# Decode rows' memory attention moved into the sixteenth projection block, and the block end ahead of the attention removed

## The reference, cut to what matters

```python
def mem_branch(p, mk, mv, dtype):
    B, L, _ = p['mem_q'].shape
    q = p['mem_q'].reshape(B, L, MEM_H, MEM_DH).astype(F32)
    s = jnp.einsum('blhd,bmhd->bhlm', q, mk.astype(F32)) * (MEM_DH ** -0.5)
    a = jax.nn.softmax(s, axis=-1)
    o = jnp.einsum('bhlm,bmhd->blhd', a, mv.astype(F32)).reshape(B, L, MEM_W)
    return (o * jax.nn.silu(p['mem_z'].astype(F32))).astype(dtype)

# for the decode rows: c_s = mem_branch(ps, c_mk, c_mv, x_s.dtype)
#   c_mk, c_mv: 8 x 256 x 4 x 128;  ps['mem_q']: 8 x 4 x 512
```

## Time and profile before

| | us |
|---|---|
| median of 3 runs | 2792.88 |
| lowest, highest | 2790.41, 2792.89 |
| the profiled execution's own time | 2791.27 |
| its span | 2789.4 |
| PE busy | 2710.3 (97%) |
| stretch from the last product of quad 15 to `dots(0)` | 39.50, PE busy 25.07 |

### The profile page before, as it was taken

One profiled execution on the slowest core, in us unless ns is written; L12 is line 12 of the kernel. 1 busy time (PEld: TensorE's weight loads), 2 busy tenths in 40 slices (PEclk: granted clock), 3 DMA queues, 4 the chain that ended last, 5 costly groups with the idle time before them and its releaser, 6 DMA issues. The chain is left out here.

```text
span 2789.4 us, 35948 instructions
## 1 busy us (share of the span) xinstructions
PE 2710.3 (97%) x13915; PEld 1927.5 (69%) x13915; DVE 1244.9 (45%) x2147; ACT 580.6 (21%) x1367; POOL 404.6 (15%) x819
## 2 busy tenths in 40 slices
PE   7998999999999999999999999999789999899998
PEld 6674468856844588888888888888655565455553
DVE  3252688867854663142222144451232232345453
ACT  3122458760000000000010100100132232122221
POOL 0000014320000000000000023320123200333341
PEclk9999999999999999999999999999899999999999
DMA  6457312212222221222342354552764411875652
GB/s 228 107 160 247 110 36 71 85 38 67 84 80 89 83 64 55 72 68 89 106 127 65 104 155 138 156 173 75 237 214 140 130 50 47 288 237 166 209 164 92
DMA packets 273463, 342.00 MB, mean 123 GB/s; under 512 B 40989, under 2 KB 226325, under 8 KB 268013
## 3 DMA queue, kind: packets, MB, share of 16 engines
q1 hardware_dynamic: 239932, 262.65, 30.1%
q0 software_dynamic: 16288, 67.46, 7.9%
q10 hardware_dynamic: 17072, 9.58, 1.1%
HBM read 262.16 MB, written 80.01 MB: 123 GB/s over the span
## 5 line engine op out<-in xcount | busy, mean ns | idle before, releaser
L1420 PE MATMUL sbank<-w,xT 128*128 128x256 f32 x3200 | 698.6, 379 | 0.0
L1420 PEld LDWEIGHTS sbank<-w,xT 128*128 128x128 f32 x3200 | 606.5, 190 | 85.0 <-issue 3.3
L1420 PE MATMUL sbank<-w,area 128*128 128x256 f32 x1664 | 361.3, 379 | 0.0
L1839 DVE TENSOR_TENSOR pout_b<-pout_b,sbank 128x256 f32<-128x256 f32 x320 | 134.2, 421 | 503.6 <-PE sbank L1420 414.8
L1420 PEld LDWEIGHTS sbank<-w,area 128*128 128x128 f32 x1664 | 315.9, 190 | 42.8
L1802 DVE TENSOR_TENSOR w<-w 128x2048 f32<-128x2048 f32 x63 | 142.8, 2288 | 320.7 <-PE sbank L1420 257.5
L1512 ACT ACTIVATE pout_b<-sbank 128x256 f32<-128x256 f32 x120 | 45.4, 384 | 890.0 <-PE sbank L1420 657.9
L1420 PE MATMUL sbank<-w 128*128 128x256 f32 x832 | 181.8, 379 | 2.6 <-issue 2.6
L1420 PEld LDWEIGHTS sbank<-w 128*128 128x128 f32 x832 | 158.0, 190 | 24.2 <-issue 2.8
L1417 PE MATMUL sbank<-xT,w 128*128 128x512 f32 x384 | 166.6, 593 | 0.0
L1417 PEld LDWEIGHTS sbank<-xT,w 128*128 128x128 f32 x384 | 72.7, 190 | 90.1 <-issue 90.0
(11 more groups left out here) (455 smaller groups left out, 3433.4 us busy)
## 6 DMA issues: line engine op xcount, KB each, us to landing
w<-in_w_in SPq DMA_DIRECT2D x64, 1024.0 KB, 5.3
proj<-pout_b SPq DMA_DIRECT2D x208, 128.0 KB, 1.7
area<-in_x_prompt SPq DMA_DIRECT2D x16, 1024.0 KB, 7.4
attention_then_units<-proj SPq DMA_DIRECT2D x128, 128.0 KB, 3.1
area<-roped_q_of_decode POOLq DMA_DIRECT2D x32, 256.0 KB, 4.1
w<-in_w_out SPq DMA_DIRECT2D x4, 2048.0 KB, 15.6
y_of_groups_b_c<-out_parts SPq DMA_DIRECT2D x32, 256.0 KB, 2.3
mo_dec_states<-in_state_mlstm_C SPq DMA_DIRECT2D x32, 256.0 KB, 5.9
```

What stands on the lines that cost most here:

```text
L1420: last = nc.tensor.matmul(bank[t][:, 0:256], x(c, t * P, (t + 1) * P), at[name][:, c, :], start=first_ and c == 0, stop=c == 7, skip_group ...
L1839: nc.vector.tensor_tensor(out[:, t, :], x[:, t, :], product_at(n, t), ALU.add).then_inc(sums_read, 1)
```

## The change

1. `select`, `attend_bc` and `mix_out` now share one block. The meeting of all engines between `select` and `attend_bc` is gone; instead SP, once the stores of quad 15 have landed except the last four, clears the stage's semaphores and increments `selected`, for which every engine waits.
2. Turning the decode rows' memory keys, their dots and the softmax move into quad 15: `decode_memory(step)`, after step 10 to 23 of it, on PE, ACT and DVE. SP loads the queries and the first four sequences' keys ahead of quad 15's stores, the other four after phase 2, and the values of all eight sequences through the rest of the quad.
3. The products with the memory values are cut in four (`memory_values(part)`), one behind `dots(s)` in each of slots 0 to 3. Slot 3's increments `closed`.
4. The decode logits and their softmax are spread over slots 2 to 5 (`decode_logits`, `decode_max`, `decode_p`, `decode_spread`); the tile is cleared in slot 0.
5. SP's queue: `load(0)` comes first, with `v` (2048 KB) and `mv` (512 KB) between its selection bias and its two gate tiles `z`; `load(1)` now stands behind the first part of `w_out`, and this behind `closed`. New ids, head mask, `qr` and `kn` go through GpSimd's queue, ahead of its gathers.

The diff, cut:

```diff
-        bank = [k.ps(f"sbank{j}", [P, 512], st) for j in range(8)]
+        bank = [k.ps(f"sbank{j}", [P, 512], st) for j in range(6)] + k.banks
...
-                sp.dma_start(dst, qout[:, t, :]).then_inc(quad_out[t], 16)
+                sp.dma_start(dst, qout[:, t, :]).then_inc(last_out if (n, kind) == (NQ - 1, 3) else quad_out[t], 16)
...
             def quad(n):
+                if n + 1 == NQ:
+                    sp.wait_ge(r_stored, 16 * N_TILES)
+                    sp.dma_start(dmq, k.headT[:, T_MQ:T_MQ + H, SEQ:TOK]).then_inc(dmq_in, 16)
+                    sp.wait_ge(dots_s, 2 * NS)
+                    for b in range(4):
+                        load_keys(b)
...
                     sp.dma_start(k.mk, outs["prompt_mem_k"].rearrange("(c p) n -> p c n", p=P)).then_inc(k.mk_in, 16)
-                    for b in range(5):
-                        sp.dma_start(k.mkd[:, b, :, :], ins["cache_mem_k"][b].rearrange("(c p) n -> p c n", p=P)
-                                     ).then_inc(k.mkd_in[b], 16)
+                    for b in range(4, DEC_B):
+                        load_keys(b)
+                    load_values(7)
...
                 if n + 1 == NQ:
-                    for b in range(2):
-                        sp.dma_start(k.mvd[:, 2 * b:2 * b + 2, :], ins["cache_mem_v"][b].rearrange("(c p) n -> p c n", p=P)
-                                     ).then_inc(k.mvd_in, 16)
+                    load_values(0)
+                    load_values(1)
...
+                if n + 1 == NQ:
+                    load_values(2)
+                    load_values(3)
+                    sp.wait_ge(mkd_turned, 5)
+                    load_values(6)
...
                 if n + 1 == NQ:
-                    sp.wait_ge(r_stored, 16 * N_TILES)
+                    load_values(4)
+                    load_values(5)
                     sp.dma_start(k.kT, k.headT[:, T_K:T_K + H, 0:SEQ]).then_inc(k.keys_in, 16)
...
-                if n + 1 == NQ:
-                    sp.wait_ge(product, 28 * n + 28)
-                    sp.dma_start(k.v, outs["prompt_v"].rearrange("(c p) n -> p c n", p=P)).then_inc(k.keys_in, 16)
...
-            stored_by(NQ)
...
+            def dots_mkd(b):
+
+                if b == 0:
+                    pe.wait_ge(dmq_set, 2)
+                pe.wait_ge(mkd_kept_a, b + 1)
+                pe.wait_ge(mkd_kept_v, b + 1)
+                for h in range(H):
+                    last = nc.tensor.matmul(bank[7][NS * h:NS * (h + 1), 0:N_MEM], dmq_of[:, h, NS * b:NS * (b + 1)],
+                                            mkdT[:, b % 2, h, :], start=b == 0, stop=b == DEC_B - 1)
+                last.then_inc(mdots, 1)
+
+            def decode_memory(step):
+
+                b = step - MEMORY_AT
+                if 0 < b <= DEC_B:
+                    dots_mkd(b - 1)
+                if 0 <= b < DEC_B:
+                    turn_mkd(b)
+                if b == DEC_B + 3:
+                    pe.wait_ge(pm_ready, 1)
+                    for c in range(2):
+                        last = nc.tensor.transpose(bank[5][:, c * P:(c + 1) * P], pmd[:, c * P:(c + 1) * P], k.ident[:])
+                    last.then_inc(pm_turned, 1)
+                if b == DEC_B + 5:
+                    pe.wait_ge(pm_set, 4)
...
+                        if n + 1 == NQ:
+                            decode_memory(4 * phase + t)
...
+                if 0 <= b < DEC_B:
+                    dve.wait_ge(mkd_turned, b + 1)
+                    if b >= 2:
+                        dve.wait_ge(mdots, b - 1)
+                    nc.vector.tensor_copy(mkdT[:, b % 2, 2:4, :].rearrange("p a b -> p (a b)"), bank[6][:, :]
+                                          ).then_inc(mkd_kept_v, 1)
+                if b == DEC_B + 1:
+                    dve.wait_ge(mdots, DEC_B)
+                    of_memory.step(nc.vector.tensor_reduce(stat[:, 0:1], bank[7][:, 0:N_MEM], AX, ALU.max))
+                    nc.vector.tensor_scalar(stat[:, 1:2], stat[:, 0:1], -SCALE, None, ALU.mult).then_inc(pm_max, 1)
+                    nc.vector.memset(flat[:, 14336:16384], 0.0).then_inc(spread_clear, 1)
...
+        @block.sync
+        def _(sp):
+            for t in range(4):
+                sp.wait_ge(quad_out[t], 64 * NQ - 16)
+            sp.wait_ge(decode_out, 64 * NQ)
+            k.clear(sp)
+            sp.sem_inc(k.selected, 1)
...
             def load(t):
                 rows, u = slice(t * P, (t + 1) * P), t % 2
+                if t == 0:
+                    sp.wait_ge(selected, 1)
                 sp.dma_start(qT[:, u, :, :], k.headT[:, T_Q:T_Q + H, rows]).then_inc(loaded[u], 16)
                 sp.dma_start(mq[:, u, :, :], k.headT[:, T_MQ:T_MQ + H, rows]).then_inc(loaded[u], 16)
+                sp.dma_start(bias[:, u, 0:(t + 1) * P], k.sel[rows, 0:(t + 1) * P]).then_inc(loaded[u], 16)
+                if t == 0:
+                    sp.dma_start(v, outs["prompt_v"].rearrange("(c p) n -> p c n", p=P)).then_inc(v_keys_in, 16)
+                    sp.dma_start(mv[:, :, :], outs["prompt_mem_v"].rearrange("(c p) n -> p c n", p=P)).then_inc(mv_in, 16)
                 for j, c in enumerate((C_SZ, C_MZ)):
                     sp.dma_start(z[:, u, j, :], k.proj[rows, c:c + HW]).then_inc(loaded[u], 16)
-                sp.dma_start(bias[:, u, 0:(t + 1) * P], k.sel[rows, 0:(t + 1) * P]).then_inc(loaded[u], 16)
-
-            sp.dma_start(dmq[:, :, :], k.headT[:, T_MQ:T_MQ + H, SEQ:TOK]).then_inc(dmq_in, 16)
-
...
-            sp.dma_start(hm[:], ins["head_pick"][:, :]).then_inc(small_in, 16)
-            sp.dma_start(qr[:], k.sq.rearrange("t (h d) -> (t h) d", h=H)).then_inc(small_in, 16)
-            sp.wait_ge(k.new_stored, 16 * 2 * DEC_T)
-            for t in range(DEC_T):
-                sp.dma_start(kn[:, t, :], k.kn4[t].rearrange("b t (h d) -> (b t h) d", h=H)).then_inc(small_in, 16)
-            for b in range(5, DEC_B):
-                sp.wait_ge(mkd_turned, b - 4)
-                load_mkd(b)
-            for t in range(DEC_T):
-                sp.dma_start(vn[:, t, :], k.vn4[t].rearrange("b t (h d) -> (b t h) d", h=H)).then_inc(vn_in, 16)
-            for b in range(2, DEC_B):
-                sp.dma_start(mvd[:, 2 * b:2 * b + 2, :], ins["cache_mem_v"][b].rearrange("(c p) n -> p c n", p=P)
...
-                             ).then_inc(mvd_in, 16)
-            sp.dma_start(mv[:, :, :], outs["prompt_mem_v"].rearrange("(c p) n -> p c n", p=P)).then_inc(mv_in, 16)
+
             load(0)
...
                 sp.dma_start(w[b], ins["w_out"][ML_W:D, cs].rearrange("(c p) n -> p c n", p=P)
                              ).then_inc(w_in[b], 16)
+                if b == 0:
+                    load(1)
+                    for t in range(DEC_T):
+                        sp.dma_start(vn[:, t, :], k.vn4[t].rearrange("b t (h d) -> (b t h) d", h=H)).then_inc(vn_in, 16)
             for s in slots:
...
+            for t in range(DEC_T):
+                nc.gpsimd.dma_start(kn[:, t, :], k.kn4[t].rearrange("b t (h d) -> (b t h) d", h=H)).then_inc(small_in, 16)
             for q in range(QUADS):
...
+            def memory_values(part):
+                if part == 0:
+                    pe.wait_ge(k.mvd_in, 16 * DEC_B)
+                for b in (2 * part, 2 * part + 1):
                     for c in range(2):
-                        last = nc.tensor.transpose(
...
-            pe.wait_ge(keys_in, 32)
-            pe.wait_ge(mv_in, 16)
+            pe.wait_ge(keys_in, 16)
             for s in slots:
                 if 1 <= s <= A_UNITS:
                     turn_p(s - 1)
                 if s < A_UNITS:
                     dots(s)
+                if s < 4:
+                    memory_values(s)
                 if group(s) is not None:
                     multiply(group(s), 0)
                 if 2 <= s <= A_UNITS + 1:
...
                     turn_h(s - 2)
                 if 1 <= s <= A_UNITS:
                     mix(s - 1)
+                if s == 3:
+                    turn_logits()
...
                     finish_m(s)
+                if s == 0:
+                    nc.vector.memset(spread[:], 0.0).then_inc(masks, 1)
+                if s == 4:
+                    memory_out()
+                if s == 2:
+                    decode_logits()
+                if s == 3:
+                    decode_max()
+                if s == 4:
+                    decode_p()
+                if s == 5:
```

More of the change, by code:

```diff
@@ L1529, in quad @@
                     keep_groups(q)
+                if n + 1 == NQ:
+                    for step in range(MEMORY_AT, 16):
+                        decode_memory(step)
                 for kind in (2, 3, 4):
@@ L1984, in _ @@
             load(0)
-            load(1)
+            sp.wait_ge(k.last_out, 64)
+            sp.wait_ge(mk_turned, 1)
             sp.wait_ge(closed, 1)
@@ L2116, in _, with turn_logits @@
-            last.then_inc(closed, 1)
+            def turn_logits():
+                pe.wait_ge(lk_ready, 1)
+                for c in range(2):
```

(24 more changed lines are left out.)

370 lines of the change are left out of this document (183 added, 187 removed).

## The result

The changed kernel takes 2808.16 us (median of 5 runs, 2803.16 to 2810.99) where the kernel before takes 2792.89 (median of 5, 2790.41 to 2797.33). The ratio is 1.0053, with a 95% interval of 1.0038 to 1.0068: slower by some 15 us. A second set of five gave 2804.83 and a ratio of 1.0045 (1.0029 to 1.0060). The profiled execution took 2803.16 us, its span is 2801.3.

A forecast was written before the change was run, and what follows sets the result against it. PE, busy for 97% of the span, was taken to bound the kernel, with DMA late in some stretches. 13.0 - 21.0 + 12.3 + 2.0 = +6.3 us gave 2797.6, and 1.6 up to the median gave 2799.2; range 2789 to 2806.

The forecast's parts named there:

- the landing of `load(0)`: Between quad 15's last product (E) and `dots(0)`: its last tile lands 16.7 us after the first issue, bounds 14.2 and 19.5.
- `load(0)` alone: SP's queue up to the last gate tile: 3648 KB at 393 GB/s, 9.5 us, some 10.1 with short rows, plus 2.3 start.
- GpSimd's small loads: Beside `load(0)`: 450 KB in 1280 short pieces add 1.8 us to its landing.
- GpSimd's gathers: 8 x 256 KB, first issued at E + 8.2, meeting up to the last 4.5 us of `load(0)` and stretching these to double.
- quad 15: Eight sequences' key transposes and dots, plus softmax-weight transposes, cost PE their full time: +13.0 us, bounds 12.9 and 14.
- last product to `dots(0)`: From E, the end of quad 15's last product, to `dots(0)`: 18.5 us against 39.5, so -21.0, bounds -23.5 and -18.2.
- slots 0 to 2, length: Memory values partly at half clock and clearing in slot 0: 16.0 us against 13.6 before, bounds 12.9 and 17.5.
- slots 4 and 5, length: Two more transposes and softmax 0.6 us, half clock after the wait 1.4: +2.0 on 9.2, bounds +0.6 and +3.3.
- The second wait: In slot 3, `dots(4)` waits for `load(1)` behind `w_out`: 13.8 us after `dots(3)`, 3.9 before; bounds 12.8 and 15.0.
- The rival without it: `load(1)` lands before PE reaches `dots(4)`, taking 7.1 us and 1.4 of half clock off: 2790.7 us, 9%.
- the one with neither wait: Gate tiles also pass `v`, so `dots(0)` comes 8 to 9 us earlier: 2782 us, 5%.
- the 9% rival: Quad 15's cover fails, or half clock reaches slot 6's products: 5 to 10 us on top, 2804 to 2809, 9%.

The follow-up runs named there:

- f2: Changed kernel with GpSimd waiting for `v` to land ahead of its seven small loads, so its gathers come late too; a single run, 2798.17 us.
- e2: Changed kernel with GpSimd's gathers of the decode values held back until `v` has landed; 2800.07 us, ratio 1.0026.
- f1: The changed kernel measured again with nothing edited; 2804.83 us, ratio 1.0045.
- e1: Changed kernel with the two gate tiles of `load(0)` issued ahead of `mv` and `v`, and `mv` ahead of `v`; 2797.46 us, ratio 1.0018.
- f3: Changed kernel with gate tiles ahead of `mv` and `v` and gathers held until `v` landed, `load(1)` still behind `w_out`'s first part; 2794.36 us, ratio 1.0001.

## Why the prediction was wrong

The forecast was 2799.2 with a range of 2789 to 2806. The direction was right, the size was not: the median of 2808.2 lies 2 us outside, 9.0 above the forecast. The second set's median of 2804.83 lies inside the range by the luck of the scatter; the same step failed there too.

**The step that failed** is the landing of `load(0)`: "Bounds: 14.2 (they miss it) and 19.5 after the first issue; I take 16.7, in the middle". It was 21.4 to 21.6 us, `dots(0)` stood at E + 23.5 and not 18.5, and the term is -16.0, not -21.0. The parts of the landing, by f2, e2 and f1:

| | predicted | measured |
|---|---|---|
| `load(0)` alone | 12.4 | 14.6 (f2) |
| GpSimd's small loads | 1.8 | 1.2 (e2 against f2) |
| GpSimd's gathers | 2.5 | 5.7 (f1 against e2) |

The gathers were taken for an overlap of the last few microseconds of `load(0)`. But SP's loads were slower, the gathers were issued at E + 6.6 and not 8.2 (the small loads take 0.56 us each to issue, not 0.9), and once they overlap, all their bytes go through the same 16 DMA engines ahead of the last tile. I had taken half of the largest overlap, and it was all of it: 14.2 + 5.5 = 19.7, about my upper bound. That the landing lies beyond the bound, too, is `load(0)` itself (2.2 us more, most of it lost at its two ends, less 0.6 for the small loads). The Trainium skill, "DMA: Bandwidth & Descriptors", section "Queues, rings and completion order", says that each DMA engine takes turns between the queues that it has work for, a packet at a time. The shares of 56.1% and 47.6% agree in that both queues were served in the same 10 us; turns of a packet no row shows. Nor does a row show small tiles overtaking a large one: `v` landed 15.9 us after its issue at 1997.85, and `dots(0)`, which waits for the gate tiles issued behind it, came 4 us later.

The other steps of the sum, against the first profiles. The kernel before scatters in these places too: its `dots(0)` stood at E + 39.5, 44.0 and 41.5, its `dots(3)` at 53.1, 55.4 and 52.9. So the 23.5 against the forecast 18.5 says more than the -16.0.

| step | predicted | measured |
|---|---|---|
| quad 15 | +13.0 | +13.0 |
| last product to `dots(0)` | -21.0 | -16.0 |
| slots 0 to 2, length | 16.0 | 15.3 (f1: 16.0) |
| `dots(3)` to `dots(4)` | 13.8 | 13.75 (f1: 13.76) |
| slots 4 and 5, length | 11.2 | 11.8 |
| from slot 6 to the end | 0 | -0.9 |
| ahead of quad 15 | 0 | +1.6 |

- *Quad 15* is right to 0.1 us, with the reason: PE busy for 103.27 of 103.30 us, clock 1.00, no late copy.
- *`load(0)` begins at E + 1.95*, 1.8 predicted. With the meeting of all engines gone, PE still stands 2.0 us for SP's clearing (L130).
- *The second wait* is there with its price: `w_out` issued 1.95 us after `dots(3)` (2.2 predicted), 7.23 us idle. The rival without it (9%) and the one with neither wait (5%) fall. No wait for `w_out` at slot 6.
- *Half clock after the waits*: the memory values took 1.94 us in slots 0 and 1 and 1.08 after that, and slots 4 and 5 ran at 0.53, so they cost +2.6 and not +2.0. The half clock ended before slot 6 and no copy was late, so the 9% rival falls. Its 2804 to 2809 us hold the median only by chance.
- *The sum* against the profiled execution: +6.3 predicted, +11.9 measured. Of the 5.6 between them 5.0 is `dots(0)`, 1.6 lies ahead of quad 15, and the other rows give back 1.0.
- *Slips in the working*: the 1.8 us for the small loads had no row behind it; 450 KB at 393 GB/s are 1.2, which is what they cost. The bound of 19.5 is 14.2 and 2048 KB at that rate (5.3), not 4.5 us doubled, which gives 18.7. The range ended at 2806, under the 2807.0 of its own upper bounds. And of the signs of being wrong none was for a `dots(0)` that comes late.
- *From the profile to the median* I added 1.6, as for the kernel before. It was 5.0 in the first set, since the profiled run was the fastest of its five. These 3.4 us are no mechanism of the change: in the second set the profiled run was the second slowest, at 2806.45 with a median of 2804.83. With +11.4 in place of +6.3 the forecast would have been 2804.3.

The range failed for both reasons: the bounds of the first landing were too narrow, and it left no room for a scatter that moves single runs of the kernel before from 2787 to 2805. Neither alone would have taken the median out of it: 2808.2 less 5.0 or less 3.4 lies inside.

## What to carry to other kernels

Where several DMA queues are busy together, count every byte that lands before the awaited tile, whoever issues it, against one rate, and add what the two ends cost. Here, at 382 GB/s, the bytes up to the last tile of `load(0)` are 9.8 us in f2, 11.0 in e2 and 16.5 in the changed kernel, and `dots(0)` came 4.8, 4.8 and 5.1 us after that. Let a prefetch that nobody needs soon wait for the tile that somebody does. Where a load is moved behind a barrier, sort the queue by first use: three small edits (two loads moved, one wait added) turned this change from 12 to 15 us slower into 10 us faster. Edits by themselves can give back part of their gain at the next late transfer (e1, f3), so try them together before judging one.
